# Four gate chunks moved between softmax units, and the weight fold in half-size steps

## The reference

```
shift, scale, gate = split(silu(c) @ ada_w[i] + ada_b[i])
h = rms_norm(x, norm_g[i]) * (1 + scale) + shift
# i = 0: q, k, v, g = split(h @ attn_w_in); q, k normed, rotated
#        branch = (banded_sink_attention(q, k, v) * silu(g)) @ attn_w_out
# i = 1: v, g = split(h @ pool_w_in)
#        mixed = einsum(pooled(v), w_group) * scale      (4 groups of 256 channels)
#        branch = (mixed * silu(g)) @ pool_w_out
x = x + gate * branch
```

## Time and profile before

| what | value |
| --- | --- |
| median of 3 runs | 1520.98 us (1518.25 to 1523.82) |
| the profiled execution | 1514.76 us, its span 1513.0 us |
| TensorE busy | 1427.6 us, 94% of the span |
| VectorE, ACT, POOL busy | 890.8, 537.3, 385.7 us |
| mean granted TensorE clock | 0.992 of full speed |
| DMA issues: at_w, at_qt | 1024 KB each |
| at_vs, at_sg, at_kt | 768, 512, 512 KB |
| at_wg_raw, at_early_wv_raw, at_x | 256 KB each |

### The profile page before, as it was taken

One profiled execution on the slowest core, in us unless ns is written; L12 is line 12 of the kernel. 1 busy time (PEld: TensorE's weight loads), 2 busy tenths in 40 slices (PEclk: granted clock), 3 DMA queues, 4 the chain that ended last, 5 costly groups with the idle time before them and its releaser, 6 DMA issues.

```text
span 1513.0 us, 20206 instructions
## 1 busy us (share of the span) xinstructions
PE 1427.6 (94%) x7240; PEld 1206.2 (80%) x7240; DVE 890.8 (59%) x1524; ACT 537.3 (36%) x1270; POOL 385.7 (25%) x551
## 2 busy tenths in 40 slices
PE   1899999999999987799999999999999999999999
PEld 1678878788778876788888888788888888888887
DVE  7777666665444447777777775625555543555522
ACT  2443443333211126675555563322222212222200
POOL 2333333321222214455555554310000100000000
PEclk9999999999999998999999999999999999999999
DMA  8655555434899776756776765831121562112142
GB/s 311 219 183 194 192 186 199 176 138 169 336 345 366 282 296 229 252 216 217 287 274 236 283 256 202 299 98 54 45 76 49 169 193 72 47 42 77 50 153 84
DMA packets 96787, 285.62 MB, mean 189 GB/s; under 512 B 10768, under 2 KB 40496, under 8 KB 87088
## 3 DMA queue, kind: packets, MB, share of 16 engines
q1 hardware_dynamic: 87760, 250.74, 46.2%
q0 software_dynamic: 8928, 33.59, 6.4%
HBM read 196.22 MB, written 88.08 MB: 188 GB/s over the span
## 4 chain that ended last, share of the span: by engine, by line
PE 72%; DVE 9%; DMA 8%; ACT 5%; issue 3%; POOL 2%; SPq 1%; ACTq 0%; DVEq 0%; POOLq 0%
PE po_f_ps L1839 23%; PE po_y_ps L1855 12%; PE at_y_ps L1411 10%; PE ga_g_ps L929 8%; PE qk_proj L663 7%; PE at_o_ps L1395 5%; PE at_s_ps L1367 3%; DMA values_split<-qk_late 3%; DMA ga_ada<-in_ada_w 2%; PE at_tr L1377 2%; ACT at_pr L1187 1%; DMA ga_raw<-in_attn_w_gate 1%; DMA po_xn<-x_mid_t 1%; POOL qk_rq L306 1%; PE qk_tr L679 1%
## 5 line engine op out<-in xcount | busy, mean ns | idle before, releaser
L1839 PE MATMUL po_f_ps<-po_ht,po_w 128*128 128x512 f32 x1536 | 349.0, 389 | 0.0
L1839 PEld LDWEIGHTS po_f_ps<-po_ht,po_w 128*128 128x128 f32 x1536 | 288.2, 188 | 60.1 <-DVE po_ht L1701 0.3
L663 PE MATMUL qk_proj<-qk_w_qkv,qk_ht 128*128 128x512 f32 x1152 | 280.3, 399 | 7.0 <-DVE qk_w_qkv L539 4.0
L663 PEld LDWEIGHTS qk_proj<-qk_w_qkv,qk_ht 128*128 128x128 f32 x1152 | 214.9, 190 | 54.0 <-issue 6.1
L1411 PE MATMUL at_y_ps<-at_zt,at_w 128*128 128x512 f32 x768 | 198.4, 400 | 3.1 <-DVE at_x L1300 3.1
L1855 PE MATMUL po_y_ps<-po_zt,po_w 128*128 128x512 f32 x768 | 174.7, 389 | 0.0
L1855 PEld LDWEIGHTS po_y_ps<-po_zt,po_w 128*128 128x128 f32 x768 | 144.1, 188 | 29.9
L1411 PEld LDWEIGHTS at_y_ps<-at_zt,at_w 128*128 128x128 f32 x768 | 138.4, 190 | 28.7 <-issue 4.1
L1688 DVE TENSOR_TENSOR po_w<-po_raw,po_w 128x1024 fp32r<-128x1024 f32 x48 | 58.8, 1225 | 128.6 <-ACT po_w L1622 128.6
L1143 POOL TENSOR_SCALAR_AFFINE_SELECT at_pt<-at_ph 128x512 fp32r<-128x512 f32 x128 | 83.3, 674 | 188.6 <-ACT at_ph L1194 188.6
L306 POOL TENSOR_TENSOR qk_rq<-qk_mq,qk_half 128x8 f32<-128x8 f32 (+1 forms) x48 | 70.3, 1464 | 177.8 <-DVE qk_mq L485 177.7
(11 more groups left out here) (168 smaller groups left out, 1956.4 us busy)
## 6 DMA issues: line engine op xcount, KB each, us to landing
at_w<-out_weight_split SPq DMA_DIRECT2D x32, 1024.0 KB, 6.2
queries_t<-qk_late SPq DMA_DIRECT2D x16, 1024.0 KB, 4.0
ga_ada<-in_ada_w POOLq DMA_DIRECT2D x64, 256.0 KB, 4.9
at_qt<-queries_t SPq DMA_DIRECT2D x16, 1024.0 KB, 8.0
ht_split<-qk_ht SPq DMA_DIRECT2D x6, 2048.0 KB, 9.6
values_split<-qk_late SPq DMA_DIRECT2D x16, 768.0 KB, 4.5
at_vs<-values_split SPq DMA_DIRECT2D x16, 768.0 KB, 4.9
qk_late<-in_ada_w SPq DMA_DIRECT2D x16, 512.0 KB, 6.1
```

The lines of the kernel that those rows point to most:

```text
L663: last = nc.tensor.matmul(proj[:, b * BANK:(b + 1) * BANK], ht[:, s % 2, m, k, t * P:(t + 1) * P], w_qkv[:, w, k, b * BANK:(b + 1) * BANK] ...
L1839: last = nc.tensor.matmul(f_ps[:, bank(j, h), :], w[:, i % 2, a, k, :], ht[:, h, m, k, :], start=(n == 0), stop=(n == 3 * KC - 1))
```

## The change

- `gate_stage` does only 28 of its 32 chunks (`DENSE`). The last four, pieces 4 to 7 of the third token group, are done by TensorE in slots 0 to 7 of the attention stage, one chunk in two slots, in four quarters of 6 matmuls (`fill_product`). All four use one bank (`FILL_BANK`). Their tanh and silu stand at the head of ACT's and VectorE's slots 2, 4, 6 and 8, through the buffer `acc`, and each is stored by itself (256 KB). The last 6 adaLN rows, the last `sum_mods` and `set_mods` move into the same slots.
- The 28 chunks use seven banks, and the output weight's pieces begin at chunk 6 instead of 8.
- A fold is now one of 32 steps v of 128 columns. Steps 0 to 19 go two to a slot in slots 9 to 18, one before and one behind the transposes; steps 20 to 31 go one to each of the output chunks 0 to 11, in its second slot. Their buffers are halved: two of `wv_raw`, of `wv` and of `folded`, one of `w_group`.
- ACT evicts the first step of a slot behind the exps of the same slot, ahead of `fold_high`, and the second at the start of the next slot. SyncE loads steps two slots ahead, each waiting for `fold_low` of the step two before. w and x for the first output chunks are loaded in slots 9 to 11.

```
-        for q in range(SLOTS):
+        for q in range(DENSE):
             gate_chunk(q)
...
+    def fill_product(pe, n, ks):
+        q, f = DENSE + n, FILL + n
+        if ks[0] == 0:
+            pe.wait_ge(silu_done, q if n > 0 else DENSE - 3)
+        for k in ks:
+            for w, m in PRODUCTS:
+                last = nc.tensor.matmul(g_bank(q), split_of(f, w)[:, k * P:(k + 1) * P], ht[(NSB - 2) % 2][:, m, k, :],
...
+    def fold_slot(v):
+        return FOLD_FROM + v // 2 if v < PAIRED else first_slot(v - PAIRED) + HALVES - 1
...
+    def load_fold(sp, v):
+        f, b = v // PER_GROUP, v % PER_GROUP
+        if v == 0:
+            sp.wait_ge(ga["g_done"], ga["slots"])
+            sp.wait_ge(weights["lo"], ga["items"])
+        if b == 0:
+            if f > 0:
+                sp.wait_ge(fold_lo, wg_split(f - 1))
+            sp.dma_start(wg_raw[:, :, :], w_group[GC * f:GC * (f + 1)].rearrange("c p n -> p c n")).then_inc(wg_loaded, 16)
+        if v >= 2:
+            sp.wait_ge(fold_lo, wv_split(v - 2))
+        sp.dma_start(wv_raw[:, v % 2], wvt[GC * f:GC * (f + 1)][:, :, b * P:(b + 1) * P].rearrange("c p n -> p c n")).then_inc(fold_loaded[v % 2], 16)
...
     def sync(sp, next_load):
         for i in range(LAST):
             m = i // KV + 1
             if 2 <= m < NB and i % KV == 0:
                 load_qk(sp, m)
...
+            for v in folds_in(i - 1):
+                store_fold(sp, v)
+            for v in folds_in(i + 2):
+                load_fold(sp, v)
+            if i in range(FILL_SLOTS + 1, FILL_SLOTS + 4):
+                load_w(sp, i - FILL_SLOTS - 1)
+                load_x(sp, i - FILL_SLOTS - 1)
...
+        def fold_evict(v):
+            act.wait_ge(fold_done, v + 1)
+            if v == 0:
+                act.wait_ge(ga["mod_set"], 3)
+            wait(act, fold_stored[v % 2], 16 * (v // 2))
...
         for i in range(LAST + 1):
+            if i in range(HALVES, FILL_SLOTS + 1, HALVES):
+                ga["fill_tanh"](act, i // HALVES - 1, acc[:, :])
             if i < UNITS:
                 previous(i)
-            if 0 <= i - 3 < FOLDS:
-                fold_evict(i - 3)
+            for v in folds_in(i - 1)[1:]:
+                fold_evict(v)
...
             if i < UNITS:
                 exps(i)
-            if i < FOLDS:
-                fold_high(i)
+            for v in folds_in(i)[:1]:
+                fold_evict(v)
+            for v in folds_in(i + 1):
+                fold_high(v)
...
+            for v in folds_in(i)[:1]:
+                fold(v)
+            fill(i, 0)
             for c, k in part:
                 output(c, list(range(k, k + quarter)))
             if 1 <= i <= UNITS:
                 p_round(i - 1)
-            if 0 <= i - 2 < FOLDS:
-                fold(i - 2, 1)
+            for v in folds_in(i)[1:]:
+                fold(v)
+            fill(i, 1)
```

More of the change, by code:

```diff
@@ new lines, in tanh, with silu @@
+    def tanh(act, q):
+        act.wait_ge(g_done, q + 1)
+        if q % KC == 0:
+            wait(act, sg_stored, 16 * (q // KC))
+        nc.scalar.activation(sg[:, :, q % KC, :], g_bank(q).rearrange("p (n t) -> p n t", n=PER), ACT.Tanh,
+                             scale=0.5).then_inc(tanh_done, 1)
+    def silu(dve, q):
+        dve.wait_ge(tanh_done, q + 1)
+        nc.vector.scalar_tensor_tensor(sg[:, :, q % KC, :], sg[:, :, q % KC, :], 1.0, g_bank(q).rearrange("p (n t) -> p n t", n=PER),
+                                       ALU.add, ALU.mult).then_inc(silu_done, 1)
@@ new lines, in sum_mods @@
+    def sum_mods(pe, j):
+        if j == 0:
+            pe.wait_ge(consts_set, 1)
+            pe.wait_ge(qk["hx_done"], KC * NB // 2)
+        pe.wait_ge(ada_added, KC * (j + 1))
+        for c in range(PER):
+            last = nc.tensor.matmul(mod_ps[:, j * PER + c:j * PER + c + 1], sums[:, j % 2, c * P:(c + 1) * P],
+                                    ones[:, 0:1], start=True, stop=True)
+        last.then_inc(mod_summed, 1)
+    def fill_product(pe, n, ks):
[5 more added lines that the diff above has]
+                last = nc.tensor.matmul(g_bank(q), split_of(f, w)[:, k * P:(k + 1) * P], ht[(NSB - 2) % 2][:, m, k, :],
+                                        start=(k == 0 and (w, m) == PRODUCTS[0]), stop=(k == KC - 1 and (w, m) == PRODUCTS[-1]))
+        if ks[-1] == KC - 1:
+            last.then_inc(g_done, 1)
@@ L931, in gate_chunk @@
             last.then_inc(g_done, 1)
-        def sum_mods(j):
-            if j == 0:
-                pe.wait_ge(consts_set, 1)
-                pe.wait_ge(qk["act_ev"], 2 * NB)
-            pe.wait_ge(ada_added, KC * (j + 1))
-            for c in range(PER):
-                last = nc.tensor.matmul(mod_ps[:, j * PER + c:j * PER + c + 1], sums[:, j % 2, c * P:(c + 1) * P],
-                                        ones[:, 0:1], start=True, stop=True)
-            last.then_inc(mod_summed, 1)
-        for q in range(SLOTS):
+        for q in range(DENSE):
             gate_chunk(q)
@@ L1334, in vector @@
                 p_lo(i - 1)
-            if i < FOLDS:
-                fold_low(i)
+            for n in ga["ada_left"][i:i + 1]:
+                ga["add_ada"](dve, n)
+            for v in folds_in(i + 1):
+                fold_low(v)
         for c in range(CHUNKS - KC, CHUNKS):
```

309 lines of the change are left out of this document (165 added, 144 removed).

## The result

The changed kernel takes 1545.2 us (median of 4 runs, 1542.4 to 1548.7) where the kernel before takes 1519.6 (1517.2 to 1523.8) beside it on the same chip: a ratio of 1.017, interval 1.015 to 1.019. It is slower, as forecast, but by 25.6 us instead of 9.5, and the time lies 4 us above the upper end of the range (1541). The profiled execution took 1544.28 us, its span 1542.6. That of before was a quick one (1514.76 us, 4.9 under its median), so the two spans lie 29.6 us apart and about 4 of these are scatter.

What follows compares the result with a forecast made beforehand. TensorE was taken as the bound nearly throughout, with an ACT and VectorE chain holding fold slots; -22.9 - 3.2 + 1.4 + 24.6 + 9.6 = +9.5 us gave 1530.5 us, range 1507 to 1541.

Steps and rivals of the forecast that it cites:

- the store waits: Slots 10, 11, 12 and 16: evictions wait for a store one slot back; +24.6 us including 1.0 for a late load.
- Rivals 1 and 2: Slots 10, 11, 12, 16: stores land in time, 1505.9 us, chance 0.20; or half the stalls, 1518 us, chance 0.15.
- The fit of the Trainium skill: Store landings: a DMA takes 2.0 us plus bytes at 436 GB/s, making the whole sum +2 us.
- My own reckoning by bytes: Slot 12's store wait: both lots in one burst, 1.25 MB more at 345 GB/s, 3.8 us more, 11.0 us wait.
- -22.9 us: Gate stage: four chunks leave it (22.07 us) and the last sum_mods group (0.8 us) moves too.
- TensorE covers them: Gate stage: other bank assignment and output weights split two chunks earlier cost nothing; otherwise 1 or 2 us.
- The prediction's own sign: End of gate stage: last gate chunk 22 to 23 us earlier; if it ends after 534.5, the gate saving is wrong.
- Rival 4: Slots 0 to 7: one bank makes filling chunks run one after another, up to +3 instead of -3.2; 1537 us, chance 0.05.
- the unstalled forecast: Slots 8 to 18 without DMA waits: rounds of 5.8 us, 63.5 us against 62.1, +1.4 us.
- Folds among output chunks: Output slots: twelve folds of six matmuls each add 0.80 us, +9.6 us; bounds 9.6 and 20.
- Lies beside TensorE: Output slots: the folds' work on ACT and VectorE, some 0.8 us each, overlaps TensorE's work.
- Rival 3: Output-chunk fold loads late in each second one (+9) and stalls a quarter longer (+6); 1545 us, chance 0.08.

## Why the prediction was right and where it was wrong

**Slower, and mainly by the store waits: right.** Forecast 23.6 us in slots 10, 11, 12 and 16, measured 25.2; the 1.0 forecast for a late fold load is a wait of 0.9 at 600.51, one slot later than said. Four buffers, which take away only the cause of the store waits, gave 18.8 us back. Rivals 1 and 2 (stores in time, half the stalls) are out. The fit of the Trainium skill ("DMA: Bandwidth & Descriptors", "Anatomy of one DMA — SWDGE (gpsimd) path") made the stalls an estimated 17 us; 25.2 were measured, so it is out too. My own reckoning by bytes met the total but not the rule, so its closeness in slot 12 is in part luck: it gave 11.0 in slot 12 for a burst with w in it, 3 of it for w, and without w the wait is still 10.7.

**Gate stage: "-22.9 us" is the step that failed.** I took it off as if slot 0 followed the last gate matmul, and what I costed at nothing ("TensorE covers them") was only the banks and the earlier splits. POOL's list was not followed past the end of the gate stage. Its constants were 6.3 us early before; with TensorE 19 us earlier (536.74 against 556.06) and the last output-weight store only 6.5 us earlier (541.20 against 547.67), they were bound to be late. The rows for this were in the trace of before. The prediction's own sign said so, too: the last gate chunk ahead of the attention stage ended at 535.94, behind the 534.5 past which the first term was to be wrong, and 19.3 us earlier than before (555.25) instead of 22 to 23. POOL's order cost 6.5 us of waiting and 1.5 at the lower clock; the run that moves the constants and the one that delays the pieces show the mechanism from both sides.

**The gate stage's other 4.7 us are not settled.** Without that wait it took 171.1 us where 189.3 - 22.9 = 166.4 was forecast. TensorE's waits in it are 5.4 us against 4.3 before, of which those for the split gate weights are 3.5 against 1.5. The larger part is the clock, by an estimate from the starts of the matmuls some 3 us more of it than before. One of the runs of matmuls between them went at a lower granted clock, and another later:

```profile
399.35 18.22 PE L975 MATMUL ga_g_ps<-qk_ht,ga_w_fill 128*128 128x512 f32 x72 [2.29 <-DVE ga_w_fill L866]
```

```profile
400.00:410.00 10.00, 10.00 (x39) 8.09 (x38) 6.67 (x9) 1.98 (x3) 2.15 (x4) 0.83 0.92 327
...
450.00:460.00 10.00, 10.00 (x38) 8.04 (x38) 5.96 (x10) 1.66 (x2) 2.94 (x6) 0.83 0.77 243
```

Before, 72 such matmuls took 16.66 us at 1.00. In the profiles of the twelve edited kernels the stage took 167.8 to 172.0 us, so 1.4 to 5.6 over the forecast, with waits of 2.1 to 4.1 us for these weights. That the output-weight pieces are the cause is not shown; why the gate weights come later, and how much of the 4.7 us is scatter of one profile against another, was not tried.

**Slots 0 to 7: mechanism right, size off by 2.4 us.** The fill chunks do wait for the bank, three times, 2.0 us in all (forecast 2.8). 1.5 us is slot 0's lower clock, which belongs to the wait ahead of it. Rival 4 (+3 instead of -3.2) is out at -0.8.

**Slots 8 to 18.** Unstalled slots are 5.72 us, forecast 5.8. 90.7 less 26.0 of ACT's waits for transfers (forecast 24.6) is 64.7; the unstalled forecast was 63.5. By the same count the other five profiles with two buffers and nothing edited in these slots come to 64.9 to 65.6, and the four kernels with four buffers, with 2.3 to 8.9 us of such waits, to 63.8 to 64.3. So what follows a long wait adds about 1 us in all here, though the slow matmuls lose more: the slot behind them is short (4.47 us).

**Folds among output chunks.** Slot by slot against the kernel before, a step adds 0.59 to 0.74 us instead of 0.80, 7.8 for the twelve (with the loads early, where none is late); its six matmuls are 0.72, but most of these slots took 5.70 us in the kernel before and not 5.61. Slot 28, with the split of the last w_group, is 1.7 us longer still, and the late loads of slots 26, 34 and 42 make 2.0. "Lies beside TensorE" held.

**Rival 3 has the number (1545) without the mechanism.** It wanted 9 us of late fold loads and 6 of longer stalls; there were 2.0 and 1.4. Nothing in my range stood for a term left out, and nearly all of the miss is such terms. Of the 20.2 us by which the spans miss, 8.0 are POOL's order (wait and clock), 4.7 the rest of the gate stage, 3.0 lie behind slot 63, 2.6 in slots 8 to 18, 1.9 in the output slots and 0.9 in the rest of slots 0 to 7, while the start gave 0.9 back; about 4 of the whole is the quick profile of before.

**Behind slot 63** the changed kernel and all twelve variants are 1.2 to 3.6 us longer than the one profile of before. TensorE waits three times instead of twice for the residual of an output chunk (at_x, 6.0 us against 3.1). No run was made for it.

## What to carry to other kernels

Where a stage is shortened, follow the list of every other engine across its end: what another engine does for the next stage doesn't get shorter with it, and the trace of before says how early it was. A wait on a DMA is to be counted in slots of slack against the landing time under load, not the quiet one; one more buffer can be worth more than any order of the list (18.8 us here against 6.7 and 7.5), and an order that only deals the same loads out over more slots paid nothing until the slack was there. Add to the price of a wait what TensorE loses afterwards at the lower clock where TensorE sets the pace, as in slot 0; where a chain over other engines does, as in slots 8 to 18, little of it shows in the time (about 1 us in all). And before a stretch of a few us is read from one profile, see how far it scatters in profiles of kernels that don't touch it.
